# Compression stage: VectorE makes all eight copies of a unit, ScalarE requests ten of its 32 pages

## The reference, cut to what matters

```
def compress_blocks(rows, pe, w1, w2):
    B, L = rows.shape[:2]
    nb = L // CMP_BLK
    blk = rows[:, :nb * CMP_BLK].reshape(B, nb, CMP_BLK, 2, NSA_KV_HEADS, NSA_HEAD_DIM)
    h = jax.nn.silu(jnp.einsum('bnlcgd,lcde->bncge', blk + pe[:, :, None, :], w1))
    return jnp.einsum('bncge,cef->bncgf', h, w2)
```

## Time and profile before

| | |
|---|---|
| median of three runs | 1758.61 us |
| the profiled execution | 1758.1 us |
| its span | 1756.4 us |
| first copies of `phase_compress` | 181.1 us |
| last products of unit 7 end | 299.4 us |
| DMA over the span | 215.47 MB, mean 123 GB/s |

### The profile page before, as it was taken

The page is one execution under the profiler, slowest core; times in us unless marked ns, Lnnn a source line. Parts: engine busy times, 40 slices in busy tenths (PEclk is TensorE's granted clock), DMA queues, the critical chain, the costliest instruction groups (busy, mean ns, idle before and its releaser), DMA issues. The chain is left out here.

```text
span 1756.4 us, 35338 instructions
## 1 busy us (share of the span) xinstructions
PE 1593.4 (91%) x13658; PEld 1407.0 (80%) x13658; DVE 757.8 (43%) x1412; ACT 643.3 (37%) x1198; POOL 740.8 (42%) x522
## 2 busy tenths in 40 slices
PE   6998477798899789999999999998979999999997
PEld 6998466566566578999999988986658899999996
DVE  2211345555455568222232276146659523223234
ACT  3221465455454335322322324136434531222323
POOL 6641452433354356544344336412136644434420
PEclk9998788799999999999999999998989999999998
DMA  8336895454354543533333322324223333233211
GB/s 240 111 87 163 277 291 159 121 178 156 113 178 151 170 133 107 180 110 119 108 121 94 87 67 67 88 88 152 60 84 98 108 109 91 86 89 105 81 32 49
DMA packets 295264, 215.47 MB, mean 123 GB/s; under 512 B 33925, under 2 KB 287417, under 8 KB 294329
## 3 DMA queue, kind: packets, MB, share of 16 engines
q1 hardware_dynamic: 279464, 180.70, 34.2%
q0 software_dynamic: 8496, 22.68, 4.0%
q10 hardware_dynamic: 7136, 9.83, 2.2%
HBM read 200.95 MB, written 20.55 MB: 126 GB/s over the span
## 5 line engine op out<-in xcount | busy, mean ns | idle before, releaser
L1719 POOL TENSOR_TENSOR w_low_t<-w_raw,w_high_t 128x1024 fp32r<-128x1024 f32 (+1 forms) x126 | 298.2, 2374 | 298.9 <-ACT w_high_t L1827 298.9
L1560 PE MATMUL ps<-x_parts,w_high_t 128*128 128x512 f32 x720 | 263.5, 404 | 16.5 <-POOL w_low_t L1719 16.0
L1807 PE MATMUL ps<-x_parts,w_high_t 128*128 128x264 f32 x720 | 205.1, 285 | 0.0
L1562 PE MATMUL ps<-x_parts,w_low_t 128*128 128x256 f32 x720 | 204.9, 285 | 0.0
L1809 PE MATMUL ps<-x_parts,w_low_t 128*128 128x264 f32 x720 | 204.4, 284 | 0.0
L1808 PE MATMUL ps<-x_parts,w_high_t 128*128 128x264 f32 x720 | 204.4, 284 | 0.0
L1827 ACT CAST w_high_t<-w_raw 128x1024 fp32r<-128x1024 f32 (+1 forms) x126 | 127.9, 1024 | 136.6 <-PE ps L1809 118.3
L1560 PEld LDWEIGHTS ps<-x_parts,w_high_t 128*128 128x128 f32 x720 | 138.8, 193 | 48.0 <-POOL w_low_t L1719 16.5
L1719 POOL TENSOR_TENSOR w_low_ahead<-w_raw,w_high_ahead 128x1024 fp32r<-128x1024 f32 (+1 forms) x40 | 95.0, 2380 | 132.6 <-ACT w_high_ahead L1827 132.6
L1562 PEld LDWEIGHTS ps<-x_parts,w_low_t 128*128 128x128 f32 x720 | 139.1, 193 | 0.1
L1807 PEld LDWEIGHTS ps<-x_parts,w_high_t 128*128 128x128 f32 x720 | 135.4, 188 | 2.9
(11 more groups left out here) (396 smaller groups left out, 4036.0 us busy)
## 6 DMA issues: line engine op xcount, KB each, us to landing
w_raw<-in_ffn_w_gu SPq DMA_DIRECT2D x88, 512.0 KB, 3.7
pages<-in_cache_slc SPq DMA_DIRECT2D x192, 128.0 KB
rows<-in_cache_cmp SPq DMA_DIRECT2D x130, 128.0 KB, 5.9
w_raw<-in_ffn_w_down SPq DMA_DIRECT2D x32, 448.0 KB, 3.6
w_raw<-in_gla_w_in SPq DMA_DIRECT2D x24, 512.0 KB, 3.7
rows<-in_cache_cmp POOLq DMA_DIRECT2D x84, 128.0 KB, 5.9
pages<-in_cache_slc POOLq DMA_DIRECT2D x64, 128.0 KB, 2.9
w_raw<-in_ffn_w_down SPq DMA_DIRECT2D x16, 512.0 KB, 3.9
```

What stands on the lines that cost most here:

```text
L1560: nc.tensor.matmul(bank[:, 0:2 * FOLD].rearrange("p (a n) -> p a n", a=2), high, parts[2][:, :, at, 0:FOLD], start=(k == 0), stop=False)
L1562: return nc.tensor.matmul(bank[:, FOLD:2 * FOLD], low, parts[0][:, at, 0:FOLD], start=False, stop=(k == n - 1))
L1719: nc.gpsimd.tensor_tensor(low(u)[:, 0:k], raw[:, u % RAW, 0:k], high(u)[:, 0:k].bitcast(F32), ALU.subtract).then_inc(low_done, 1)
L1807: nc.tensor.matmul(psum(i), high(u)[:, k, :], a[0][:, at, c], start=(k == 0), stop=False)
```

## The change

Three things are changed. Shares: SyncE requests 13 pages a unit, ScalarE 10, GpSimd 9. Copies: VectorE makes all eight of each unit, and ScalarE keeps the sigmoids, the scores' copy and its requests; its sigmoid of unit n - 1 now stands at the top of unit n in the code, behind the request for unit n + 1. In `phase_project` `pe` is requested ahead of `w1`.

```
-ROW_SHARE = (0, 14, 20, ROW_UNIT)
+ROW_SHARE = (0, 13, 23, ROW_UNIT)
...
-                    act.dma_start(w1[64 * hf:64 * hf + 64, c], io["nsa_w_cmp1"][0, :, c]).then_inc(cst["w1_in"][c], 16)
+                    act.dma_start(S["pe_cmp"][64 * hf:64 * hf + 64, c], io["nsa_pe_cmp"][0, :, c, :]).then_inc(cst["rows0_in"], 16)
             for c in range(2):
                 for hf in range(2):
-                    act.dma_start(S["pe_cmp"][64 * hf:64 * hf + 64, c], io["nsa_pe_cmp"][0, :, c, :]).then_inc(cst["rows0_in"], 16)
+                    act.dma_start(w1[64 * hf:64 * hf + 64, c], io["nsa_w_cmp1"][0, :, c]).then_inc(cst["w1_in"][c], 16)
...
             if n >= 2:
-                eng.wait_ge(flat_act, CH // 2 * (n - 1))
-                eng.wait_ge(flat_dve, CH // 2 * (n - 1))
+                eng.wait_ge(flat_dve, CH * (n - 1))
...
             for n in range(len(UN)):
-                for j in range(0, CH, 2):
-                    flatten(act, nc.scalar.copy, n, j, flat_act)
-                    if j == 2 and n:
-                        sigmoid(n - 1)
+                if n:
+                    sigmoid(n - 1)
...
-                for j in range(1, CH, 2):
+                for j in range(CH):
                     flatten(dve, nc.vector.tensor_copy, n, j, flat_dve)
...
-                    pe.wait_ge(flat_dve if j % 2 else flat_act, k // 2 + 1)
+                    pe.wait_ge(flat_dve, k + 1)
```

More of the change, by code:

```diff
@@ L488, in phase_compress @@
         w2_in, pm_in = sem("w2_in"), sem("pm_in")
-        flat_act, flat_dve, chunk_done, other_done, pre_done, sig_done, hid_done = (
-            sem(n) for n in ("flat_act", "flat_dve", "chunk_done", "other_done", "pre_done", "sig_done", "hid_done"))
+        flat_dve, chunk_done, other_done, pre_done, sig_done, hid_done = (
+            sem(n) for n in ("flat_dve", "chunk_done", "other_done", "pre_done", "sig_done", "hid_done"))
         bias_done, ck_done, ckx_done = sem("bias_done"), sem("ck_done"), sem("ckx_done")
@@ L527, in flatten @@
             dst = flat[k % RING]
-            if j < 2:
+            if j == 0:
                 rows_there(eng, n)
@@ L583, in _ @@
                     act.wait_ge(cst["cmp_out"], 16 * 4)
-                    act.wait_ge(flat_dve, CH // 2 * len(EX))
+                    act.wait_ge(flat_dve, CH * len(EX))
                     for g in range(G):
```

## The result

The changed kernel takes 1762.98 us (median of 20 runs, 1759.75 to 1770.88), the kernel before in the same comparison 1759.21 (20 runs). The ratio is 1.0021, 95% interval 1.0013 to 1.0030: 3.8 us more. The interval leaves out 1, and 3.8 us is just over the 3.5 that was to count as a difference, so the change made the kernel a little slower. The profiled execution is one of the slower ones, 1765.4 us with a span of 1763.7, which is 2.4 above the median; before it was 1758.1 and 1756.4. So the two traces are 7.3 us apart, the medians 3.8.

The account below looks back on a forecast made before the run. TensorE waits 43.7 us for copies, nearly always ScalarE's; page loads of 16.1 us a unit are the second limit. 216.2 + 84.1 = 300.3 against 299.4, +0.9 us on 1758.1: 1759.0, range 1751 to 1766.

Parts of the forecast that it names:

- the high edge: Slow end of the forecast's own range, 1755 to 1763 us; together with the second rival given 0.22.
- the second rival: ScalarE's page requests take 0.8 us each, sigmoids behind them: 9.4 us more, 1768; decides from about 0.6; chance 0.16.
- The first three steps: Stage start at 176.2 us, unit 1's pages arriving at 204, unit 1's copies ending at 216.2.
- the steady part: Units 2 to 7, from F(1) to unit 7's last products: 84.1 us in place of 87.6, 3.5 shorter.
- F(0): End of unit 0's copies: 186.7 us, from a start at 176.2 and eight parts, 10.4 us.
- The overtaking: Unit 2's early-requested pages share the DMA engines before SyncE's queue finishes unit 1, which arrives at 204, before 195.7.
- the first rival: No overtaking at unit 1: pages arrive at 196 whatever the queue order, 7.1 us earlier end, 1751; chance 0.28.
- F(1): End of unit 1's copies: 12.2 us after its last page arrives, 216.2 us; later units are counted from it.
- F(2): End of unit 2's copies: 15.6 us behind F(1), its sigmoid standing behind ScalarE's ten requests and ten lookups.
- F(3): End of unit 3's copies: 27.1 us behind F(1), its sigmoid behind ScalarE's requests without lookups.
- the prediction's own signs: Wrong if unit 0 begins at 181, VectorE's copies exceed 1.06 us, or 32-page loads take other than 16 us.
- the last eighth: Unit 7's final part is multiplied 1.1 us after its copies end at 83.0, so 84.1 behind F(1).

Follow-up runs that it names:

- x1_table: The kernel before with only the positional table requested ahead of w1, old shares and copies on both engines: 1764.34 us, ratio 1.0031 to the kernel before.
- x2_shares: The changed kernel with the old page shares 14, 6, 12, VectorE still making all copies and the table first: 1760.09 us, ratio 1.0006 to the kernel before.
- x4_gate: The changed kernel with ScalarE and GpSimd requesting unit 2's pages only after SyncE's pages of unit 1 landed: 1756.14 us, ratio 0.9982 to the kernel before.
- x5_no_table: The changed kernel with the positional table requested behind w1 again: 1755.04 us, ratio 0.9964 to the kernel before.

## Why the prediction came out as it did

The time, 1763.0, lies in the range, at the upper edge of the forecast's own (1755 to 1763). The forecast was 1759.0 and no change (0.48); what came is a small slowdown, by the high edge and not by the second rival (together 0.22). The first three steps came out to 0.3 us, in part by luck; the steady part was 5.8 us too short in the profiled execution. That execution is 7.3 us above the one before, and the medians are only 3.8 apart: that the median came within 4 us of the forecast is partly luck too.

**The start.** 176.2 was predicted, 176.16 measured. F(0) was 186.7, and is 186.77. That the figure agrees so well is in part luck: in the variants with the table first the stage began between 174.0 (`x1_table` and `x2_shares`, with fewer lookups) and 177.1, and in `x4_gate`, with the same code ahead of it, at 174.7.

**Unit 1's pages.** 204 was predicted, 203.75 measured. The overtaking is shown by `x1_table` and `x4_gate`. So the first rival (196) is out: the sum of the queues is the same, and yet the arrival depends on when the others are asked for theirs. The way to 204 was not right in detail. GpSimd's own nine requests last until 189.5, since VectorE's copies hold them. I had q0 share the engines evenly from 181 on; it moved 0.39 MB from 182 to 186, 0.01 from there to 190, and then took more than a third. So q1 was quicker at first, 2.37 MB from 181 to 199 where I had 1.9, and 0.106 MB/us holds for it only from 190 to 202. It had moved as many bytes as its line for unit 1 held, 2.75 MB, between 201 and 202 (2.67 by 201, 2.81 by 202), but the last page of unit 1 landed at 203.73, and for that the sum had no term. These errors cancelled: the mechanism was right, the agreement to 0.3 us is luck. F(1) was 216.2 in both. The prediction had the table's price in it, 4.9 us won and 8 lost, but did not say that the other two edits alone would be faster; `x5_no_table` shows that they are.

**Units 2 and 3.** The sigmoid behind ten requests and ten lookups was predicted with F(2) = 15.6 us behind F(1) and measured at 17.1. The term mis-sized is the ten requests, 6.51 us where I took 4.9 from the quicker of two rows. The other tens from `phase_compress` took 5.33 to 6.84, 0.53 to 0.68 us each. The second rival's 0.8 and its sign, ten requests in over 7 us, did not occur; but the five tens of units 2 to 6 took 0.62 us each on average, just over the 0.6 from which I had said it decides, and 0.06 more than the forecast had. F(3) was 27.6 for 27.1.

**Unit 4.** 43.0 predicted, 45.1 measured. I had let ScalarE decide, with pages at 31.8 behind F(1). They came at 251.44, 35.2 behind it: 18.0 us after their request, not 16.1. Unit 5's pages were asked for 10.5 us after unit 4's, so they shared the engines. One of GpSimd's requests also took 6.92 us (below). Which of the two made the 1.9 us no run separates. Unit 7's pages took 17.3 us in place of 16.3. By the prediction's own signs this is a fault in it: it called itself wrong if a load took other than 16 us with the new shares. The wait of 3 us for the sigmoid that it gave unit 4 did not come either, since the pages were later.

**Unit 5.** 57.2 predicted, 62.2 measured, the largest miss; 2.1 of the 5.0 us came over from unit 4. I had 0.7 us for the scores' transposes on TensorE. TensorE after, and the stretch of it (busy time of PE, PEld, DVE, ACT, POOL, then granted clock):

```profile
270.48 3.67 PE L733 MATMUL ps<-ident,sT 128*128 128x128 f32 x16 [4.27 <-ACT sT L584]
```

```profile
270.00:274.00 4.00, 3.52 (x16) 3.27 (x16) 2.34 (x3) 0.85 (x2) 0.00 (x0) 0.50 1.06 356
```

Sixteen transposes took 3.67 us at a granted clock of 0.50, the lower of the two levels, after TensorE had stood idle 4.27 us for the scores' copy. Before, the same sixteen took 1.97 us at 1.00. There the low clock had fallen on the products ahead of them: 64 of these took 3.36 us, after an idle of 3.00, and the clock from 264 to 266 was 0.54. So a pause with the low clock behind it was there before, too; now it falls on the transposes. The scores' copy itself had begun at 268.37, behind ten requests of 6.84. VectorE's ring then waited 2.89 for TensorE, and `finish` 3.53 for the sigmoid. The forecast took each engine alone; in unit 5 ScalarE, TensorE and VectorE wait in turn, one for the other, and that was missed.

**Units 6 and 7.** 11.6 us and 14.9 were measured where 11.7 and 14.1 were predicted, and the last eighth ended 1.2 later where 1.1 was foretold. In all 89.9 for 84.1. The sum was 300.3 and is 306.04, and behind it the time is as before to 0.7 us.

**The gain.** ScalarE's 62.4 us of copies are gone, and they were what TensorE waited for the earlier trace rows. VectorE makes them in 31.0 us more than its own took (64.9 for 33.9), but it now waits 17.0 us for unit 1's pages, 10.7 for sigmoids and 9.2 for later pages. With the first two mended, the same idea is 0.7% faster than the kernel before.

## What to carry to other kernels

Taking an engine's main work off does not free what stands in its queue: look at what is left there in order, requests and lookups too, and who waits for the last of it; here moving ten lookups behind one sigmoid was worth 8.3 us, twice what the change had lost. A stage that starts earlier also asks sooner for the data after next, and these can delay the data it needs next: beginning unit 0 4.5 us sooner made unit 1 8.5 us later. Of an edit with three parts, work out the sum with each part left out, too.

## What the runs showed of the hardware

A DMA request on GpSimd can be held while VectorE copies back to back from SBUF to SBUF, for several copies on end. In the changed kernel (one instruction, then the five after it):

```profile
236.94 6.92 POOL L510 DMA_DIRECT2D rows<-in_cache_cmp  x1
```

```profile
243.85 2.65 POOL L510 DMA_DIRECT2D rows<-in_cache_cmp  x5
```

```profile
237.56 2.03 DVE L538 COPY flat<-rows 128x1024 f32<-128x1024 f32 x2
239.51 0.41 DVE L672 TENSOR_TENSOR hid<-c_pre,c_sig 64x256 f32<-64x256 f32 x1
239.84 3.90 DVE L538 COPY flat<-rows 128x1024 f32<-128x1024 f32 x4
```

The request ends at 243.86, 0.12 us after VectorE's last copy; the next five take about 0.53 each, while VectorE makes nothing but a few copies of 64x8 elements. At 181.86 another took 5.03 us and ended at 186.89, 0.12 behind unit 0's last copy. With a reduce in place of the copy the longest was 0.673 us. The hold spanned six copies and an instruction between them, not one. Not every request is held: in the changed kernel the median of the 63 is 538 ns. The Trainium skill, page "SBUF — State Buffer", section "Who interferes with whom", says that a copy of VectorE can take the port pair that it shares with GpSimd while `tensor_reduce` never does, and the two traces agree. The copies themselves took 1053 ns for 1024 elements a partition, and a reduce of the same 1903.

The clock: sixteen transposes took 3.67 us at a granted clock of 0.50, after an idle of 4.27, and 1.97 before the change at 1.00, when TensorE came to them from products without a pause.

The queues: a queue's part of the DMA engines depends on what the others have to move. In the changed kernel q1 moved 0.75 MB from 186 to 190, beside q10 alone, and 0.46 from 190 to 194, when q0 moved 0.80.
